# A new SBUF layout for a two-block transformer kernel: small vectors first, large tiles at multiples of 1024 bytes

## What is computed

```python
def reference(x, c, ctx, c_ctx, ...):
    for i in range(2):                                   # first block
        sh1, sc1, g1, sh2, sc2, g2 = ada_params(c, ada_w[i], ada_b[i])
        ax = modulate(rms_norm(x, norm_mix[i]), sh1, sc1)
        yx = retention_mixer(ax, ac, ...) if i == 0 else conv_mixer(ax, ...)
        x = x + g1 * yx
        fx = modulate(rms_norm(x, norm_ffn[i]), sh2, sc2)
        x = x + g2 * ((silu(fx @ w1[i]) * (fx @ w3[i])) @ w2[i])
    x = rms_norm(x, final_norm)
    h = rms_norm(x, mix_pre_norm)                        # second block
    mixed = concatenate([gated_delta_net(h @ w_in), mla(h @ w_in)]) @ w_out
    x = x + rms_norm(mixed, mix_post_norm)
    f = square(relu(rms_norm(x, ffn_pre_norm) @ w_up)) @ w_down
    return x + rms_norm(f, ffn_post_norm)
```

## Time and profile before

| | us |
|---|---|
| median of 3 runs | 2310.68 (2309.46 to 2317.5) |
| the profiled execution, as timed | 2306.89 |
| its span from the first to the last instruction | 2305.2 |
| TensorE busy | 2211.3 (96%) |
| VectorE busy | 1142.9 (50%) |
| ScalarE busy | 725.2 (31%) |
| GpSimd busy | 29.5 (1%) |
| DMA traffic | 231.92 MB, mean 101 GB/s |

### The profile page before, as it was taken

The page is one execution under the profiler, slowest core; times in us unless marked ns, Lnnn a source line. Parts: engine busy times, 40 slices in busy tenths (PEclk is TensorE's granted clock), DMA queues, the critical chain, the costliest instruction groups (busy, mean ns, idle before and its releaser), DMA issues.

```text
span 2305.2 us, 25545 instructions
## 1 busy us (share of the span) xinstructions
PE 2211.3 (96%) x9848; PEld 1753.7 (76%) x9848; DVE 1142.9 (50%) x1450; ACT 725.2 (31%) x958; POOL 29.5 (1%) x60
## 2 busy tenths in 40 slices
PE   6999999999899999999999999999999987999996
PEld 4868687686688888878878888888758875888885
DVE  7644344444677333273662332347778647422424
ACT  3222131211433222241342212235555634323321
POOL 0000000000011000000000000000000000000000
PEclk7999999999999999999999999999899999999998
DMA  7232322323277232222222222222101111222230
GB/s 318 73 124 78 136 73 73 123 73 123 73 276 293 105 106 95 92 83 100 91 84 99 91 92 94 107 89 93 72 1 37 38 37 58 107 91 92 91 108 38
DMA packets 32751, 231.92 MB, mean 101 GB/s; under 512 B 3760, under 2 KB 4016, under 8 KB 5552
## 3 DMA queue, kind: packets, MB, share of 16 engines
q1 hardware_dynamic: 23904, 171.98, 21.0%
q0 software_dynamic: 6912, 50.33, 5.8%
q10 hardware_dynamic: 1872, 8.73, 1.0%
HBM read 228.93 MB, written 2.10 MB: 100 GB/s over the span
## 4 chain that ended last, share of the span: by engine, by line
PE 88%; DVE 7%; ACT 2%; issue 1%; DMA 1%; ACTq 0%; DVEq 0%; POOL 0%; POOLq 0%
PE PS L478 25%; PE PS L480 25%; PE PS L479 25%; PE PS L601 4%; PE PS L592 2%; DVE rv L1680 1%; DVE w_lo L1577 1%; PE PS L881 1%; PE PS L975 1%; PE PS L846 1%; PE PS L965 1%; DVE cv L2088 1%; DMA ada_raw<-ada 1%; DVE normed L1596 1%; PE PS L812 1%
## 5 line engine op out<-in xcount | busy, mean ns | idle before, releaser
L1577 DVE TENSOR_TENSOR w_lo<-raw,w_hi 128x2048 fp32r<-128x2048 f32 x162 | 371.1, 2291 | 644.3 <-ACT w_hi L1105 644.3
L478 PE MATMUL PS<-act_hi,w_hi 128*128 128x512 f32 x1600 | 635.3, 397 | 28.4 <-DVE act_lo L1590 14.6
L1105 ACT ACTIVATE w_hi<-raw 128x2048 fp32r<-128x2048 f32 x162 | 310.1, 1915 | 1115.2 <-PE PS L480 1105.2
L480 PE MATMUL PS<-act_hi,w_lo 128*128 128x512 f32 x1600 | 630.4, 394 | 0.0
L479 PE MATMUL PS<-act_lo,w_hi 128*128 128x512 f32 x1600 | 629.9, 394 | 0.0
L478 PEld LDWEIGHTS PS<-act_hi,w_hi 128*128 128x128 f32 x1600 | 303.0, 189 | 102.2 <-issue 27.8
L479 PEld LDWEIGHTS PS<-act_lo,w_hi 128*128 128x128 f32 x1600 | 302.9, 189 | 67.7 <-issue 1.9
L480 PEld LDWEIGHTS PS<-act_hi,w_lo 128*128 128x128 f32 x1600 | 302.6, 189 | 66.1
L478 PE MATMUL PS<-hid_hi,w_hi 128*128 128x512 f32 (+1 forms) x672 | 263.9, 393 | 1.0 <-ACT sg L1538 0.9
L480 PE MATMUL PS<-hid_hi,w_lo 128*128 128x512 f32 (+1 forms) x672 | 263.1, 392 | 0.0
L479 PE MATMUL PS<-hid_lo,w_hi 128*128 128x512 f32 (+1 forms) x672 | 262.6, 391 | 0.0
(11 more groups left out here) (377 smaller groups left out, 2301.1 us busy)
## 6 DMA issues: line engine op xcount, KB each, us to landing
raw<-slabs SPq DMA_DIRECT2D x162, 1024.0 KB, 4.7
ada_raw<-ada POOLq DMA_DIRECT2D x44, 1024.0 KB, 5.1
early_raw<-ada POOLq DMA_DIRECT2D x4, 1024.0 KB, 21.0
toep<-decay ACTq DMA_DIRECT2D x5, 768.0 KB, 4.5
x<-x_t ACTq DMA_DIRECT2D x1, 2048.0 KB, 9.4
out_t<-x SPq DMA_DIRECT2D x4, 512.0 KB, 2.6
rs<-ctx_t ACTq DMA_DIRECT2D x1, 1024.0 KB, 13.9
con<-consts ACTq DMA_DIRECT2D x1, 642.0 KB, 3.9
```

The source lines that it names most:

```text
L478: pe.matmul(o, w[0], a[0], start=first, stop=False)
L480: return pe.matmul(o, w[1], a[0], start=False, stop=last)
L1105: act.activation(w_hi[:, n % 2, :], raw[:, n % 2, :], ACT.Copy).then_inc(w_hi_done, 1)
L1577: dve.tensor_tensor(w_lo[:, k % 2, :], raw[:, k % 2, :], w_hi[:, k % 2, :].bitcast(F32), ALU.subtract).then_inc(w_lo_done, 1)
```

## The change

Only the order and the size of allocations change. No instruction, wait or queue is added, removed or moved; the shapes of all operands stay.

- The ten small buffers come first. Behind them a buffer of 144 columns (576 bytes, never used) fills up to 19,456, a multiple of 1024. From there on `raw`, `w_hi`, `w_lo`, `x`, `std`, `rstd`, `normed`, `acc`, `act_hi`, `act_lo` and all tiles of the retention and of the feed-forwards start at multiples of 1024.
- `xg_hi` and `xg_lo` get rows 528 columns apart (2112 bytes, a multiple of 64) instead of 514. `u` keeps its 514.
- In the mixing block `csn` moves up to stand behind `gate`, and 16 columns (64 bytes) fill up behind the small tiles. The tiles of the attention and of the delta rule then start 256 above a multiple of 1024, so at multiples of 128. `cvin` moves to the end of the attention's tiles, with rows 528 columns apart.

```diff
 N_ADA = 48
+PAD, PAD_MIX = 144, 16
...
-        raw = sb("raw", [P, 2, SLAB])
-        w_hi = sb("w_hi", [P, 2, SLAB], F32R)
-        w_lo = sb("w_lo", [P, 2, SLAB], F32R)
-        x = sb("x", [P, KT, T])
         vec = sb("vec", [P, N_VEC])
...
         shift_sum = sb("shift_sum", [P, 2])
+        sb("to_kilobyte", [P, PAD])
+        raw = sb("raw", [P, 2, SLAB])
+        w_hi = sb("w_hi", [P, 2, SLAB], F32R)
+        w_lo = sb("w_lo", [P, 2, SLAB], F32R)
+        x = sb("x", [P, KT, T])
         std = sb("std", [P, T])
...
-                xg_lo = sb("xg_lo", [P, KT, T + 2], F32R, scaled_x)
+                xg_lo = sb("xg_lo", [P, KT, T + 16], F32R, scaled_x)
...
-                    xg_hi = sb("xg_hi", [P, KT, T + 2], F32R, scaled_x)
+                    xg_hi = sb("xg_hi", [P, KT, T + 16], F32R, scaled_x)
...
                 gate = sb("gate", [P, GH, T], F32, mix)
+                csn = sb("csn", [P, T], F32, mix)
...
-                csn = sb("csn", [P, T], F32, mix)
                 small = sb("small", [P, 3, 4], F32, mix)
+                sb("to_line", [P, PAD_MIX], F32, mix)
                 with ExitStack() as mla:
-                    cvin = sb("cvin", [P, 4, T + 3], F32, mla)
...
                     pr2 = sb("pr2", [P, 2, T], F32, mla)
+                    cvin = sb("cvin", [P, 4, T + 16], F32, mla)
```

## The result

The changed kernel takes 2295.16 us (median of 5 runs, 2292.82 to 2295.94) against 2310.84 us before (5 runs, 2309.46 to 2317.5). The ratio is 0.9921, with a 95% interval from 0.9903 to 0.9938: faster by 0.8%. Two of the five runs before stand at 2317 us and none of the five after above 2296, so the ratio, which is taken over all runs, comes to 18.3 us and the medians to 15.7. The direction was forecast, the size was not: 15.7 or 18.3 us instead of 38.

The account below looks back on a forecast made before the run. TensorE bounds the kernel; 32.4 us (moving activations), 5.2 (moving slabs), 0.4 (256 columns) and 0.3 (scaled rows) make 38 us, giving 2272.7 us. Range 2237 to 2343 us; likeliest case 2255 to 2290.

Parts of the forecast that it names:

- What bounds the kernel: Whole kernel: TensorE, busy 96% of the span and 88% of the chain; layout acts only through its instructions' speed.
- The comparison of 228.9 with 233.3: 512-column float32r matmuls, moving activations against moving slabs: the 4.5 ns between their pitches shows that operand position matters.
- One step down for each operand: 512-column float32r products: 4.5 ns less per operand put in place, 32.4 us for moving activations, 5.2 us for moving slabs.
- The 192 matmuls with 256 columns: `ctx_hi` products: 2.2 ns less for each matmul, 0.4 us saved.
- The scaled rows: Matmuls on scaled x, 192 of them: 0.1 to 0.4 us gained, 0.3 us in the sum.
- the 15.6 ns: Moving activations, 512 columns: the part of the 228.9 ns pitch that would remain without a cause if the pitch stayed.
- A: Float32r products: only the stationary operand's position matters, moving activations stay at 228.9 ns; 2308 us; chance 0.33.
- B: Float32r products: a moving operand at a multiple of 128 is slow, all 7200 go to 233.3 ns; 2343 us; chance 0.22.
- C: Float32r products: the supply limit goes away, only a fresh stream's 6.7 ns remain; 74 us saved, 2237 us; chance 0.08.
- Plain float32 takes two cycles per column: Plain float32 matmuls: 111 ns each at different operand places, within 2.5 ns of their columns; so 0 change.
- the fresh stream's 113.3 ns: Start of a float32r stream: 6.7 ns above the bare columns, giving 220.0 ns as a nearer lower bound for 512 columns.

Follow-up runs that it names:

- all_64_off: Kernel before with small vectors first and no filling, rows of 514; slabs and large tiles start 448 above a multiple of 1024; ratio to before 0.9927.
- tiles_up_64: Kernel before plus 64 bytes of filling behind the small vectors, so only the tiles move, to 512 above a multiple of 1024; ratio 1.0105.
- scaled_rows: Kernel before with only the row stride of scaled x changed from 514 to 528 columns; ratio 1.0001.
- all_128_only: As all_64_off with 64 bytes of filling: slabs and large tiles start 512 above a multiple of 1024; ratio to before 0.9929.
- tiles_up_192: Kernel before plus 192 bytes of filling behind the small vectors, so only the tiles move, to 640 above a multiple of 1024; ratio 0.9924.
- tiles_up_128: Kernel before plus 128 bytes of filling behind the small vectors, so only the tiles move, to 576 above a multiple of 1024; ratio 1.0104.
- The last kernel of its own: Separate kernel, stretches of 72 matmuls: one place repeated or two in turn, also plain float32 and bfloat16; float32r turns 64 bytes apart: 231.8 and 233.3 ns.
- the second kernel of its own: Separate kernel, stretches of 48 matmuls with separate places for high and low parts, other widths and orders; at 512 columns none beats 226.7 ns.

## Why the prediction was right in direction and wrong in size

**What bounds the kernel: right.** What changed is the pitch of TensorE. VectorE's and ScalarE's means stayed within the 5 ns that the prediction allowed, the DMA landings went from 4.7 and 5.1 us to 4.7 and 5.0, and plain float32 kept its rows.

**The comparison of 228.9 with 233.3: right to look at, wrongly read.** It was taken as one step of 4.5 ns for each operand that lies 64 bytes off a multiple of 128. The two orders do not differ in how many operands are misplaced, but in the sign of one difference: d = 64 against d = 192. One pair of rows could not tell the two readings apart; all_64_off, with both operands "misplaced", runs at the good 226.7 ns, and tiles_up_64, with both "in place", at 232.3. The step that failed is therefore the cost of an operand by its own place; what the runs show in its stead is a cost of the distance between the two. That the direction came out right is luck: the change put both operands at multiples of 128 and also made their distance 0. By the same reasoning tiles_up_64 would have been forecast 38 us faster, and it is 24 to 26 us slower.

**The term of the sum: mis-sized.** "One step down for each operand" gave 4.5 ns to 7200 matmuls and 9.0 ns to 576. Measured: 228.9 - 226.7 = 2.2 ns and 233.3 - 226.9 = 6.4 ns. So 7200 x 2.2 = 15.8 us instead of 32.4, and 576 x 6.4 = 3.7 instead of 5.2. The 192 matmuls with 256 columns went the other way: 96 x 2.0 ns in the first two heads and 96 x 6.5 in the last two, 0.8 us lost where 0.4 were to be gained. The scaled rows gave nothing: the stretch of 30 that the prediction read went from 118.7 to 120.3 ns, all that ran at full clock from a mean of 119.4 to 119.3. Together 18.7 us instead of 38. The lowest pitch for 512 columns that any run has, 13.3 ns above the columns, was not among the rows; the prediction's values between 220.0 and 224.4 assumed that placement could take away more of the 15.6 ns than it did. Of the rest no run tells the cause; bfloat16 doesn't have it.

**From 18.7 us to the 11.6 us between the two profiled spans.** The ratio says more than these two executions do: 0.9921 of 2310.8 us is 18.3 us less, with an interval from 14.3 to 22.4, and 18.7 lies in it. The medians say 15.7 us, and 14.3 to 15.8 for the other kernels with d = 0. Why these two executions show less can be placed by subtracting, from the timelines, the starts of matmuls with the same number. The distance grows steadily by the steps above, except at three places, where the kernel after loses some 2 us each against that: near 610, 1640 and 1860 us. With 0.7 us at the start this leaves 18.7 - 6.1 - 0.7 = 11.9, against the 11.6 that are to be explained. In each of them the low clock (granted share 0.50) lasts longer. Rows of the kernel before, of scaled_rows (whose pitches are those of before), and of the kernel after:

```profile
609.20:612.60 3.40, 3.40 (x8) 1.00 0.24 34
1641.40:1655.10 13.70, 13.70 (x56) 0.50 0.21 77
1868.70:1872.10 3.40, 3.40 (x24) 1.00 0.00 0
```

```profile
609.20:612.60 3.40, 3.40 (x5) 0.50 0.36 108
1643.40:1657.10 13.70, 13.70 (x53) 0.50 0.23 77
1868.70:1872.10 3.40, 3.40 (x12) 0.50 0.00 0
```

```profile
605.20:608.60 3.40, 3.40 (x5) 0.50 0.34 89
1629.20:1646.30 17.10, 17.10 (x70) 0.50 0.17 61
1857.90:1861.30 3.40, 3.40 (x13) 0.50 0.00 0
```

Two of the three can't be put down to the change: scaled_rows has the low clock there as well, and its time can't be told from before; all_64_off, with d = 0, lacks the one near 1860. The profiled execution of before was merely granted the full clock at two places where those of scaled_rows and of the changed kernel weren't. The middle one does go with the change: all five profiled kernels with d = 0 (the changed one twice, all_64_off, all_128_only, tiles_up_192) are at 1.2 GHz for 17.1 us at the start of the attention, and the four with another d (before, scaled_rows, tiles_up_64, tiles_up_128) for 13.7. 3.4 us more at half the speed are 1.7 us of full-speed work given back. Why a faster stream is held at the low clock longer there was not tried.

**The rivals.** A (only the stationary operand counts) falls, since the moving activations' pitch did move, and with all_64_off and tiles_up_64 its reason falls too. In time it came nearer than the forecast: 2308 is 13 us too high, 2272.7 is 22 us too low. B had the right thought and the wrong sign. "Two streams that start at the same place disturb each other" is the mechanism, the distance between two operands, but the same place is the fast one. The price that B named is real, though: tiles_up_64 and tiles_up_128 are 1% slower, 24 us by the ratios. C (the limit goes away) falls: 226.7 is the lowest of all places that ran with 512 columns.

**Two rows were misread.** "Plain float32 takes two cycles per column" rests on counting records. The last kernel of its own shows two records for each plain float32 matmul: 24 matmuls took the 20.60 us, 858 ns each, four cycles per column. The conclusion (no visible overhead, so nothing to gain) stood all the same. And the fresh stream's 113.3 ns, read as a reserve used up, is a value that 256 columns also hold over whole stretches: at d = 192, and in the third and fourth head of this very kernel at its own d = 64. It was no evidence of a lower floor for 512 columns, and it was the only one that the prediction had.

## What to carry to other kernels

When float32r matmuls follow each other without a gap, measure the pitch against the distance between the two operands' start addresses modulo 256, and choose it for the width that does most of the work: equal places for 512 columns. Alignment to 128 or 1024 bytes was worth nothing of its own here; a kernel whose buffers all start at multiples of 128 can be on either side by 1%. One pair of rows that differ in two things shows that something matters and not what: before costing it per operand, find the second reading (here the sign of a difference) and give it its own price.

## What the runs showed of the hardware that was not expected

- The pitch of float32r depends on (moving start - stationary start) modulo 256, signed: 226.7, 228.9, 232.1 to 233.3 and 233.3 ns at 0, 64, 128 and 192 with 512 columns; 120.0, 117.7, 118.8 (in the second kernel of its own) and 113.3 ns with 256. The best distance for 512 columns is the worst for 256.
- The same place can have two steady pitches: 256 columns at 64 ran at 117.7 ns in two heads of the kernel before and at 113.3 in the other two.
- With 512 columns a distance of 8 or 32 bytes costs as much as one of 192 (233.3 ns). The one case in which the moving operand started at 4 bytes (d = 132) is the slowest that ran with one place for high and low, 239.9 ns.
- bfloat16 (215.8 ns) and plain float32 (858.3 ns for a matmul, in two records) show no effect of place, at the six and the four distances that ran.
- Moving low alone 64 bytes out of place (232.2 ns) is dearer than both moving parts out of place by the same 64 bytes (228.9 ns).
